# Gate columns in fp32 column groups at the front, and the last FFN group written out, in a hybrid decoder layer

## The reference

```
h = RMSNorm(x); z = h @ w_in            # 3848 columns: A (gated MLP), B (window attention), C (mLSTM), 8 gate columns
x = x + concat(A, B, C) @ w_out
z2 = RMSNorm(x) @ w_up                  # 2 x 5632 columns, halves g and a
zc = conv_b + sum_j z2[t + j] * conv_w[j]   # causal, width 3, along the tokens
x = x + (silu(zc_g) * zc_a) @ w_down
```

## Time and profile before

| | us |
|---|---|
| median of three runs | 2355.12 |
| the profiled execution | 2353.2 |
| its span, from the first to the last instruction | 2351.5 |
| PE busy | 2282.0 (97%) |
| DVE, ACT, POOL busy | 865.2, 732.2, 948.6 |
| mean granted clock of TensorE | 0.979 of full speed |

### The profile page before, as it was taken

The page is one execution under the profiler, slowest core; times in us unless marked ns, Lnnn a source line. Parts: engine busy times, 40 slices in busy tenths (PEclk is TensorE's granted clock), DMA queues, the critical chain, the costliest instruction groups (busy, mean ns, idle before and its releaser), DMA issues.

```text
span 2351.5 us, 45182 instructions
## 1 busy us (share of the span) xinstructions
PE 2282.0 (97%) x18446; PEld 2205.7 (94%) x18446; DVE 865.2 (37%) x1431; ACT 732.2 (31%) x1259; POOL 948.6 (40%) x743
## 2 busy tenths in 40 slices
PE   8999999888999999999999999999999999999987
PEld 7999887777789999999999999999999999999987
DVE  6112234464444443342333324243333424333332
ACT  4222232134434432332323223232222323232232
POOL 4443333142224444444444444444444444444431
PEclk9999999789999999999999999999999999999999
DMA  5532222532213332323323232232323222232323
GB/s 171 163 89 72 73 74 71 60 105 85 68 55 89 91 92 90 95 92 97 94 89 91 89 91 89 89 91 90 98 93 96 89 89 91 89 91 89 89 72 99
DMA packets 323040, 213.45 MB, mean 91 GB/s; under 512 B 12612, under 2 KB 296893, under 8 KB 322045
## 3 DMA queue, kind: packets, MB, share of 16 engines
q1 hardware_dynamic: 315883, 210.00, 29.4%
q10 hardware_dynamic: 7092, 2.52, 1.3%
HBM read 201.37 MB, written 11.49 MB: 91 GB/s over the span
## 4 chain that ended last, share of the span: by engine, by line
PE 90%; issue 4%; DVE 3%; POOL 2%; ACTq 1%; ACT 0%; DMA 0%; DVEq 0%; SPq 0%; POOLq 0%
PE ps L422 52%; PE ps L739 22%; PE ps L641 8%; POOL wlo L1669 2%; DVE nvar L400 1%; PE ps L679 1%; PE ps L699 1%; PE ps L689 1%; PE ps L387 1%; PE ps L799 0%; PE ps L506 0%; PE ps L542 0%; ACTq L963 0%; PE ps L515 0%; PE ps L514 0%
## 5 line engine op out<-in xcount | busy, mean ns | idle before, releaser
L1669 POOL TENSOR_TENSOR wlo<-raw,whi 128x512 fp32r<-128x512 f32 x704 | 919.6, 1309 | 1332.4 <-ACT whi L842 1332.2
L842 ACT ACTIVATE whi<-raw 128x512 fp32r<-128x512 f32 x712 | 447.3, 631 | 1291.4 <-PE ps L422 846.6
L422 PE MATMUL ps<-h_hi,whi 128*128 128x260 f32 x2816 | 395.1, 282 | 0.0
L422 PE MATMUL ps<-h_lo,whi 128*128 128x260 f32 x2816 | 393.5, 282 | 0.0
L422 PE MATMUL ps<-h_hi,wlo 128*128 128x260 f32 x2816 | 393.3, 282 | 0.0
L422 PEld LDWEIGHTS ps<-h_hi,wlo 128*128 128x128 f32 x2816 | 360.9, 188 | 0.0
L422 PEld LDWEIGHTS ps<-h_lo,whi 128*128 128x128 f32 x2816 | 360.6, 188 | 0.0
L422 PEld LDWEIGHTS ps<-h_hi,whi 128*128 128x128 f32 x2816 | 359.7, 188 | 0.4
L1600 DVE TENSOR_TENSOR xT<-ps,xT 128x520 f32<-128x520 f32 x160 | 111.9, 699 | 287.9 <-PE ps L739 286.6
L739 PE MATMUL ps<-g_lo,whi 128*128 128x260 f32 x1408 | 199.5, 284 | 0.0
L739 PE MATMUL ps<-g_hi,whi 128*128 128x260 f32 x1408 | 199.3, 284 | 0.0
(11 more groups left out here) (309 smaller groups left out, 1917.2 us busy)
## 6 DMA issues: line engine op xcount, KB each, us to landing
raw<-in_w_up SPq DMA_DIRECT2D x88, 1024.0 KB, 5.3
raw<-in_w_down SPq DMA_DIRECT2D x44, 1024.0 KB, 4.9
raw<-in_w_in SPq DMA_DIRECT2D x30, 1024.0 KB, 5.2
raw<-in_w_out SPq DMA_DIRECT2D x64, 256.0 KB, 3.4
x_spill<-xT SPq DMA_DIRECT2D x1, 4160.0 KB, 16.4
xtok<-in_x_prompt SPq DMA_DIRECT2D x4, 1024.0 KB, 8.2
out_y_prompt<-ytok SPq DMA_DIRECT2D x4, 1024.0 KB
xT<-x_spill SPq DMA_DIRECT2D x1, 2860.0 KB, 9.7
```

What stands on the lines that cost most here:

```text
L422: mm = nc.tensor.matmul(ps[:, bank + h, 0:NH], w[:, k, c, :], x[:, 4 * c + k, h * NH:(h + 1) * NH], start=(k == 0 and kind == 0 and c == 0 ...
L842: nc.scalar.activation(whi[:, k, :, :], rawq(k, slot), ACT.Copy)\
L1669: nc.gpsimd.tensor_tensor(wlo[:, k, :, :], rawq(k, u), whi[:, k, :, :].bitcast(F32), ALU.subtract).then_inc(w_lo, 1)
```

## The change

- The gates: `wg_raw` is loaded first on ScalarE's queue, ahead of the gains. VectorE multiplies it by the gain into `wgs` (16 tiles of 128x32, zeros beyond column 8). TensorE multiplies it in plain fp32 with `xT`, four column tiles at a time into four groups of 32 output rows, first the half of tokens 0 to 255, then 256 to 519; the four partial sums are copied to `gsum` and added by one more matmul with a 0/1 matrix `gsel` behind unit 0.
- The gains are turned after token block 1, and block 2 waits for them. The sums of squares of x go to ScalarE (blocks 0, 2 and the sample) and VectorE (blocks 1, 3). Unit 0's tiles wait for each of their operands by kind. The norm is turned ahead of the third tile of unit 1. The ring of PSUM banks for x has 5 places instead of 6.
- The last FFN group isn't in the loop: its 8 up units run in a row, then the 16 down tiles of the group before, then its own 16. Its gated tiles have places of their own, `e_hi` and `e_lo`; `ytok` moves to the room of `h2`.
- The tails: 8 transposes of 11 channel tiles each (110 rows out), all behind the second down unit of the group before, 2 reads, and 10 stores in pieces of 512 bytes.
- y_sample is turned in four parts, each behind every fourth tile of y, with a small read each. y_prompt's last 512 columns are stored in pieces of 2, 1 and 1 tiles.

Its core:

```diff
-        pe.wait_ge(wg_lo, 1)
+        turn_x(0)
+        turn_x(1)
+        pe.wait_ge(vec_in, 16 * 8)
+        nc.tensor.transpose(ps[:, 5, P:P + 42], vrow[0:42, :], ident[0:42, 0:42]).then_inc(vec_tr, 1)
+        turn_x(2)
+        pe.wait_ge(wg_ready, 1)
...
+        gates_mm(0, (0, 1))
+        turn_x(3)
...
+        gates_mm(0, (2, 3))
...
+        gates_mm(1, range(4)).then_inc(g_part, 1)
...
+        def gates_mm(h, rounds):
+            a, b = ((0, 2 * P), (2 * P, N))[h]
+            for r in rounds:
+                for q in range(4):
+                    mm = nc.tensor.matmul(ps[32 * q:32 * q + 32, 6 + h, 0:b - a], wgs[:, 4 * r + q, :],
+                                          xT[:, 4 * r + q, a:b], start=(r == 0), stop=(r == 3))
...
         for k in range(4):
-            pe.wait_ge(h_lo, 4 * (k + 1))
-            tile_mm(k, 4, whi, wlo)
+            tile_mm(k, 0, whi, wlo, ready=ready)
+        pe.wait_ge(g_copied, 1)
+        for h in range(2):
+            mm = nc.tensor.matmul(ps[0:36, 4 + h, 0:NH], gsel[:], gsum[:, h * NH:(h + 1) * NH], start=True, stop=True)
...
-        for c in K_ORDER:
+        for i, c in enumerate(K_ORDER):
             nc.scalar.activation(act_hi[:, c, :], xT[:, c, :], ACT.Copy, scale=vecs[:, G1 + c:G1 + c + 1]).then_inc(h_hi, 1)
+            if i % 4 == 0:
+                q_hi(i // 4, i // 4, 0, 16)
...
+            if idx == 7:
+                dve.wait_ge(vec_tr, 1)
+                nc.vector.tensor_copy(vecs[:, 0:42], ps[:, 5, P:P + 42]).then_inc(vec_ev, 1)
+                dve.wait_ge(wg_in, 16)
+                tt(wgs[:, :, 0:S], wg_raw[:], vecs[:, G1:G1 + KC]..., mult).then_inc(wg_ready, 1)
+            if idx == 11:
+                square(1)
...
+        def turn_tail():
+            pe.wait_ge(z_free, U_FFN + 8 * NG + 2)
+            for r in range(2 * FC // TT):
+                tails = ztail[:, TT * r:TT * r + TT, :].rearrange("p t s -> p (t s)")
+                t = nc.tensor.transpose(ps[0:TROWS, 2 + r // 4, (r % 4) * P:(r % 4 + 1) * P], tails, ident[:])
+            t.then_inc(s("t_turn"), 1)
...
+        last = NG - 1
+        q0, use0 = 4 * U_LAST, last * 8 + U_FFN
+        up_units(q0, use0, 0, None, (last, last * 16 - 16))
+        for j in range(1, GC):
+            up_units(q0 + 8 * j, use0, j)
+        for m in range(GC):
+            for _ in down_mm(q0 + 4 * (U_GRP + m), last * 16 + 4 * m - 16):
+                pass
+            if m == 1:
+                turn_tail()
+        pe.wait_ge(s("g_lo"), NG * GC)
         for m in range(GC):
-            for k in down_mm(4 * (U_ALL - GC + m), (NG - 1) * 16 + 4 * m):
+            for k in down_mm(q0 + 4 * (U_GRP + GC + m), last * 16 + 4 * m, e_hi, e_lo):
                 if 4 * m + k >= 1:
                     turn_y(4 * m + k - 1)
-                    turn_tail(next(tails))
...
+        sp.wait_ge(s("t_read"), 2)
+        for row in range(S + 2):
+            store(sp, dst.rearrange("(r t n) -> t r n", t=TT, n=P), trow[row:TROWS:S + 2, :, :])
+        for first, tiles in ((0, 4), (4, 4), (8, 4), (12, 2), (14, 1), (15, 1)):
+            sp.wait_ge(s("y_read"), first + tiles)
+            store(sp, io["y_prompt"][0, :, cols].rearrange("(j p) d -> p j d", p=P), ytok[:, :, cols])
```

More of the change, by code:

```diff
@@ L728, in up_mm, with down_mm @@
                 tile_mm(k, bank, whi, wlo, h2_hi, h2_lo)
-        def down_mm(q0, d0):
+        def down_mm(q0, d0, x_hi=g_hi, x_lo=g_lo):
             for k in range(4):
@@ L735, in down_mm @@
                 b = 4 + 2 * (k % 2)
-                for kind, (w, x) in enumerate(((whi, g_hi), (whi, g_lo), (wlo, g_hi))):
+                for kind, (w, x) in enumerate(((whi, x_hi), (whi, x_lo), (wlo, x_hi))):
                     for c in range(4):
@@ L1161, in ffn_group_act @@
                 due.setdefault(hi_at, []).append((gated_hi, j))
-            for u in range(1, units + 1):
+            for u in range(1, units + (0 if ends else 1)):
                 for k in range(4):
                     q_hi(q1 + (4 * (u - 1) + k), k, u % 2, pair0 + 16 * (u // 2))
+                    if ends and (u, k) == (U_GRP + 3, 0):
+                        read_tail()
                     for step, j in due.get((u, k), []):
@@ L1210, in _, with square @@
         dve.nop().then_inc(z_free, 2)
+        dve.nop().then_inc(w_used, 4)
+        link(nc.vector.memset(wgs[:], 0.0))
         nc.vector.memset(rel33[32:33, :], NEG).then_inc(s("rel_set"), 1)
         link(nc.vector.memset(small[:], 1.0))
+        def square(i):
+            link(nc.vector.tensor_tensor_reduce(out=xtok[:, i, :], in0=xtok[:, i, :], in1=xtok[:, i, :], scale=1.0,
+                                                scalar=0.0, op0=mult, op1=add, accum_out=small[:, i:i + 1]))
         for idx in range(1, 16, 2):
@@ L1230, in _ @@
                 op0=mult, op1=sub).then_inc(h_lo, 1)
-        for i in range(NB + 1):
-            n = P if i < NB else S
-            link(nc.vector.tensor_tensor_reduce(out=xjunk[0:n, :], in0=xtok[0:n, i, :], in1=xtok[0:n, i, :], scale=1.0,
-                                                scalar=0.0, op0=mult, op1=add, accum_out=small[0:n, i:i + 1]))
+        dve.wait_ge(x_in[3], 16)
+        square(3)
+        dve.wait_ge(s("x_sq"), 3)
         nc.vector.tensor_scalar(small[:, 8:13], small[:, 0:5], 1.0 / D, EPS, mult, add).then_inc(var_v, 1)
@@ L1545, in _, with ffn_group_dve @@
         link(nc.vector.reciprocal(rs2[:], rs2[:]))
-        def ffn_group_dve(u0, n0, d0, base, tail, with_down):
+        def ffn_group_dve(u0, n0, d0, base, tail, with_down, ends=False):
             told = [0]
@@ L1593, in lo @@
                 dve.wait_ge(s("g_hi"), n + 1)
-                tt(g_lo[:, j, :], gm[:], g_hi[:, j, :].bitcast(F32), sub).then_inc(s("g_lo"), 1)
+                lows, highs = (e_lo, e_hi) if ends else (g_lo, g_hi)
+                tt(lows[:, j, :], gm[:], highs[:, j, :].bitcast(F32), sub).then_inc(s("g_lo"), 1)
             def down(m, k):
                 e = 4 * m + k
-                dve.wait_ge(w_used, u0 * 4 + (4 * (2 + m) + k + 5))
+                dve.wait_ge(w_used, u0 * 4 + (4 * ((U_GRP if ends else 2) + m) + k + 5))
                 x2 = halves(xT[:, e, :])
@@ L1642, in _ @@
         pool.wait_ge(const_made, 1)
-        nc.gpsimd.memset(whi[:].rearrange("p q c n -> p (q c n)").bitcast(F32), 0.0).then_inc(ring_zero, 1)
-        nc.gpsimd.memset(wlo[:].rearrange("p q c n -> p (q c n)").bitcast(F32), 0.0).then_inc(ring_zero, 1)
+        link(nc.gpsimd.memset(gsel[:], 0.0))
+        for rows in range(2):
+            cols = ident[:].rearrange("p (q m) -> p q m", q=4)[:, :, 4 * rows:4 * rows + 4]
+            to = gsel[:, 32 * rows:32 * rows + 4]
+            link(nc.gpsimd.tensor_tensor(to, cols[:, 0], cols[:, 1], ALU.add))
+            for q in (2, 3):
+                link(nc.gpsimd.tensor_tensor(to, to, cols[:, q], ALU.add))
+        pool.sem_inc(s("gsel_made"), 1)
         link(nc.gpsimd.memset(pairones[:], 0.0))
```

245 lines of the change are left out of this document (129 added, 116 removed).

## The result

| | before | after |
|---|---|---|
| median of the runs | 2355.0 us (2350.9 to 2355.8, 4 runs) | 2330.0 us (2328.3 to 2331.4, 4 runs) |
| profiled execution, its span | 2353.2, 2351.5 | 2329.7, 2328.0 |
| mean granted clock of TensorE | 0.979 | 0.982 |

The change makes the kernel about 1% faster: the ratio is 0.9897, with a 95% interval from 0.988 to 0.9914. Predicted were a median of 2328.7 us and a gain of 26.4 us in the profiled execution; measured are 2330.0 and 23.5. The gain splits unevenly over the stretches.

What follows compares the result with a forecast made beforehand. TensorE is busy 97% of the span, so only removed matmuls, holes and the two ends give time: 9.0 + 5.5 + 9.4 at the end plus 2.5 at the front, 26.4 us, forecast a median of 2328.7, range 2318 to 2336.

Steps and rivals of the forecast that it cites:

- Part 1: Last FFN group written out: the 10.64 us hole goes, less a 0.75 stall and 0.9 of tail turns, gaining 9.0.
- Part 2: Last 16 down tiles: 15 tail turns and the lower-clock start go, three groups of y_sample turns come in, gaining 5.5 us.
- Part 3: Ending after the last matmul: 6.4 us (2.2 + 3.4 + 0.8) instead of 15.8, gaining 9.4.
- Part 4: Front, up to unit 1's end: gate unit replaced by narrow matmuls in four column groups, gaining 2.5 us, bounds -2 and 14.
- The reading of the two queues: Front loads: at most one small packet passes between two of 8 KB on each DMA engine, so gains land near 16.5.
- Rival A: Front: small transfers come in time, first act_hi starts at 19 instead of 25, front gains 8.5, time 2322.7; chance 0.25.
- an op of GpSimd waits until VectorE leaves a gap: Unit 0's weight splits: few gaps, so the last split ends 18.8 us after the first act_hi starts; bounds 12 and 20.
- 2 us for restarts at the lower clock: Front, in the sum up to unit 1's end, 36.4 us after the first act_hi: 2 us for TensorE restarting at lower clock.
- rival C: Front gates: four column groups run one after the other, 10.5 us more on PE instead of 3.5 in all; 2335.2; chance 0.07.
- No change between the ends: Middle, between front and last group: the loops' bodies stay as they are, so 0 us.
- Rivals B: End gives less: down tiles stall on VectorE or short-row stores drain slowly, gain 17 + 2.5, time 2335.6; chance 0.15.
- D: Last group's straight-line code: instruction fetching slows each tile; at 0.5 us a tile the time is 2360.7; chance 0.03.

Runs made afterwards that it cites:

- 88 turns: The changed kernel with one turn for each of the 88 channel tiles of the tails, in the place of the eight: 2337.42 us, 0.9926.
- changed, again: The changed kernel run once more, nothing edited: 2327.86 us, 0.9893 of the kernel before.
- last store whole: The changed kernel with the last 512 columns of y_prompt in one store instead of pieces of 2, 1 and 1 tiles: 2331.69 us, 0.9905.
- front alone: The kernel before with only the front's edits (column groups, squares on two engines, norm inside unit 1), the old end: 2353.51 us, 0.9997.
- the gains first: The changed kernel with the load of the gate columns issued behind the eight loads of gains on ScalarE's queue: 2322.8 us, 0.9872.
- the end alone: The kernel before with only the edits behind the mixers (last FFN group, tails, y_sample), the old front: 2328.95 us, 0.9898.
- both repairs: The changed kernel with gate columns loaded behind the gains and GpSimd's splits of unit 1 held until all act_lo are written: 2320.61 us, 0.9858.
- x first: On top of both repairs, everything that does not lead to act_hi moved behind it: 2321.02 us; with ten idle matmuls in unit 1 as well: 2319.85 us.

## Why the prediction was right or wrong

The three parts at the end are right with their mechanisms. That the median is only 1.3 us off owes something to luck. The end gave 1.1 more than predicted, and two steps that were wrong, in the front and in the middle, took 4 together; the profiled execution is 2.9 off (2329.7 against 2326.8). And 1.9 us were carried over from a profiled execution to the median, of which 0.3 came.

**Part 1, right.** Predicted were 10.64 - 0.75 - 0.9; the stall is 0.47, the turns 0.87, and 9.3 us are gained. The add came later than TensorE wanted it, behind the instructions that were named. 88 turns in the same place cost 8.7 more, so the turning in elevens carries the saving.

**Part 2, right, 0.5 small.** The rounds are 3.32, where 3.33 were predicted. The last of the 15 turns of y stands behind the last tile, beside the ending's add, and was counted among the rounds (0.44).

**Part 3, right.** The ending takes 6.1 against 6.4. The last store is issued 2.19 behind the last matmul (2.2 predicted), and the span ends 3.9 later, where 3.4 and 0.8 were allowed; the load of 256 KB was a fair row for the store. With 1 MB stored at once 1.8 more are needed.

**Part 4, near only since errors cancel.** The gain is 0.9 where 2.5 were predicted, and 0.4 to 1.9 in the five profiles with this front (the column of unit 4: changed, again, 88 turns, last store whole, front alone). The working itself came to no gain (61.4 against 61.4 today); 2.5 was a choice between that and 6.8. The first act_hi at 25.84 (25 predicted) came late for another reason than the one given. The text had the gains land at 16.5, behind the gate columns, and TensorE wait for them between token blocks 1 and 2. It took the queue as something that only delays landings. In fact the issue itself took long: ScalarE stood 10.07 us in two small loads, and TensorE waited 5.14 for its reads of x inside block 1, and 0.3 for the gains, which landed near 18. The failed step is that the transfers were worked out for the data alone and not for the engine that issues them. The run with the gains first shows it: the same work, 3.7 us earlier. The reading of the two queues, one small packet for each large one, held: from 6 to 12 us each moved 335 packets. Rival A (small transfers come in time) is false for the gate columns, which land near 15.7 in either order, but the gains, when they stand ahead of them, cost nobody a wait.

The second failed step is "an op of GpSimd waits until VectorE leaves a gap". In the new order the four splits of unit 0 start at once and end near 37.8, 11.9 after the first act_hi where 18.8 was predicted. The 6.8 us that this should have given did not come, since the other engine pays: act_lo take 1.07 instead of 0.68, and these pace unit 0. Unit 0 ends at 45.90, 20.1 after the first act_hi, where 19.8 were predicted for splits that wait: nearly the same number by another path. Each split beside the act_lo costs VectorE nearly 1 us: fifteen of them take 13.93 with four splits, 15.98 with six and 17.01 with seven, and would take 10.1 at 0.68 each. A split itself grows only from 1.29 to between 1.37 and 1.66, and only beside the square of 2.28 is it as long as 3.15. The row that misled was four splits beside squares. The Trainium skill (GPSIMD Engine Reference, "1. Specifications") says that GpSimd's access to SBUF is shared with VectorE's instructions of two SBUF inputs; holding GpSimd back (15.98 to 13.93) agrees.

The third is a term of the sum, 2 us for restarts at the lower clock in units 0 and 1. There were none: from 20 to 61 us the granted clock is 1.00, although TensorE waits up to 1.6 us at a time, and from the end of unit 0 to the end of unit 1 it takes 14.7 us where 16.6 were counted. This is what made the front a little faster than today's.

The gates' price was right, 3.9 us with 3.5 predicted (3.7 if the 0.454 us a record of the earlier trace rows is put in for the 0.427 of the text), and rival C is out. The Trainium skill (TensorEngine Tiling (Array Packing), "Theoretical Speedup") gives up to four times for 32 columns; 16 records of 256 columns in 1.0 us, where eight of 512 took 3.63 alone, agree: 0.063 us a record. Half of an eighth of 3.63 is 0.227, so one group would take 3.6 times as long.

**No change between the ends, wrong.** The text priced clock restarts at the front and at the hole, and none where TensorE is always busy. The profile of before, on which the sum stands, keeps its clock up to 350 us; the changed kernel's falls at 180 and 276 us, and between the ends it loses 2.35. It isn't the change's doing as such: the end alone loses 1.4 with the old front, the changed kernel run again 1.6. The front alone loses 1.3 of its 1.8 in the same way, and what is left is too small for its medians. Predicted gain 26.4, measured 23.5: 1.6 of the 2.9 missing is the front, 2.35 the middle, and the end gives 1.1 back.

Rivals B and D are out: the end gives 25.0 in all, and a tile of the written-out group takes 2.87 (2.88 in the last rounds), as in the loop.

**The best version** is the change with both repairs, 2320.6 us (0.9858, 0.9841 to 0.9874), 7 to 9 below the changed kernel's two medians; the two "x first" kernels and, by the intervals, the gains first alone can't be told from it.

## What to carry to other kernels

Order the loads of one queue by who needs them and by their number of rows: here a load of 2048 short rows held the issue behind it for some 10 us, and with it the compute of the engine that issues. Where GpSimd and VectorE both read SBUF, ask which of the two paces TensorE, and hold the other back. The holes and tails at this kernel's end were worth what the rows said to within 0.5 us for each part, while a gain of 2 us at the front of a program of 2.3 ms can be lost in where TensorE's clock falls. So compare medians over several runs before you believe such a gain.

## What was not expected of the hardware

- Two loads of 8 KB needed 10.07 us to issue behind one of 2048 rows of 32 bytes on the same queue, and 0.90 when they stood first.
- VectorE's two-input instructions of 0.68 us took 1.07 on average beside GpSimd's splits, nearly 1 us more for each split, and the splits 1.44 to 1.66 instead of 1.29.
- The granted clock falls to its lower level with TensorE busy all the time (12 us of 12: clock 0.86 and 93 records, or 1.00 and 110), each time at a price of about 1.5 us. It falls behind rows of matmuls with few columns or with half the input rows, and not each time: three profiles with one front had it at the same two places, a fourth, whose front was 1 us earlier, at one of them and two others.
